# Sparse attention: index columns projected first, index scores and top 64 beside the other columns, probabilities scaled on POOL

## The chip, the cores and the metric

The kernel runs on one core of one Trainium2 chip. The metric is the device time of one execution in microseconds. The chip's engines are called as in the profile: PE (matrix), DVE (vector), ACT (scalar, activation), POOL (GpSimd), SP (which issues most DMAs). Each works through its own queue in order, and they meet on semaphores.

## What is computed

The reference is two transformer parts, one after the other. The change touches one stage of the second: the mixer `dsa_mixer` of its odd layer, for 256 tokens of width 1024, in float32. It projects the normed input to 2120 columns, rotates parts of them, and keeps 64 of up to 256 keys for each query by an index score:

```python
q, k, v, qi, ki, wi = jnp.split(proj, C_SPLITS, axis=-1)   # 1024, 256, 256, 512, 64, 8 columns
q = partial_rope(q.reshape(Bt, L, N_HEADS, HEAD_DIM), ...)  # 8 heads of 128; the first 32 are rotated
k = partial_rope(k.reshape(Bt, L, N_KV_HEADS, HEAD_DIM), ...)
qi = partial_rope(qi.reshape(Bt, L, IDX_HEADS, IDX_DIM), ...)  # 8 index heads of 64; the first 16
ki = partial_rope(ki, ...)
logits = relu(einsum('bthd,bsd->bths', qi, ki))
score = einsum('bths,bth->bts', logits, wi)                # causal mask, then top 64
_, idx = lax.top_k(score, topk)
s = q . k_sel * HEAD_DIM ** -0.5 ; pr = softmax(s) ; o = pr . v_sel
```

Only q, k and v pass through the attention itself. qi, ki and wi serve the choice of keys alone.

## The kernel before

The program is a list of stages. Each stage gives one function per engine, and `meet` makes all engines wait for each other between two stages. There is no scheduler: the order on an engine is the order in which the code is written. `sparse_attention` is the stage in question. Before and after it stand FFN stages whose time is PE's.

**Columns.** The weights come in six ring slots (`C_SLOTS`), five of 384 columns (`C_TILE`) and a last one of 256, of which 56 were in the slot before already. They are in the reference's order: q, k, v, then qi, ki, wi. To keep float32 accuracy with fp32r matmuls, each weight is split: ACT writes the high part (`high`, L1900, in two halves of four 128-row chunks), DVE the low part as a difference (`lows`, L1955), and PE makes three products for each chunk and each block of 128 tokens (L1836). So a slot is 48 matmuls. ACT copies the two finished banks (L1919) and only then makes the high part of the slot after next.

**Rotation and turning.** When all columns are copied, DVE rotates q and k (six steps of 320 elements, L1981 to L1986) and then qi and ki (six of 144), and copies ki twice side by side (L1987, L1988). Then PE transposes all 15 blocks (L1846), and ACT and DVE copy them out of PSUM by turns (L1928, L1992).

**Index and top 64.** PE makes 16 index matmuls (L1856), ACT a relu of each (L1935), DVE a weighted sum (L2000). Then for each token block DVE takes eight rounds of max and match_replace (L2008, L2009) and makes of that the additive mask `keep` (L2010, L2011).

**Head loop.** `skewed` overlaps eight heads. For a head PE makes the scores (L1863). DVE scales them and adds the mask in one pass over 512 elements (L2019), reduces to the maximum (L2022) and negates it (L2023). ACT takes the exponential with the sum on the side (L1939), DVE the reciprocal (L2029) and scales the probabilities (L2031, two of 256). PE transposes them (L1873), DVE copies (L2036), PE makes the outputs (L1883), ACT copies them (L1944). Then PE adds the residual (L1218) and the output projection (L779). POOL has no work in this stage. `pe.drain().then_inc(k.slot_freed, C_SLOTS)` behind the last column gives the six slots back, on which SP's next loads wait.

## Time and profile before

| | us |
|---|---|
| median of 3 runs | 2827.76 (2825.07 to 2828.39) |
| the profiled execution | 2824.92 |
| its span | 2823.2 |
| PE busy | 2254.3 (80%) |
| DVE busy | 878.9 (31%) |
| ACT busy | 593.7 (21%) |
| POOL busy | 63.1 (2%) |

The page's shares are means over very different stages: in the experts' part the weights' DMA sets the pace, in the FFN stages PE. What a change of one stage is worth has to be read in that stage: from its windows (busy time of each engine in a stretch), from the timeline (rows of one engine in order of time; a bracket gives the idle time before a row and who ended it), and from the chain of work that ended last.

### The profile page before, as it was taken

The page shows a single profiled execution, that of the slowest core. Times are in us where ns is not written, and L with a number is a line of the kernel's source. Part 1 is how long each engine was busy: PE and PEld are TensorE (multiplying, and loading weights), DVE is VectorE, ACT ScalarE, POOL GpSimd, SP SyncE. Part 2 cuts the span into 40 slices and gives each one's busy share as a digit, 9 for nine tenths or more (in the row PEclk, how much of TensorE's full clock was granted, in tenths as well). Part 3 has the DMA queues.
Part 4 walks back from the last instruction along what each step waited for, and adds up shares of the span by engine and source line. Part 5 has one row for each costly group of instructions (what it writes and reads, how often), then busy time and mean ns, then how long its engine had stood idle before and what let it go on. Part 6 is the DMA issues. An engine that isn't in the chain of part 4 may idle for free.

```text
span 2823.2 us, 35407 instructions
## 1 busy us (share of the span) xinstructions
PE 2254.3 (80%) x14966; PEld 1415.6 (50%) x14966; DVE 878.9 (31%) x1479; ACT 593.7 (21%) x964; POOL 63.1 (2%) x58
## 2 busy tenths in 40 slices
PE   6967776666767766776676899967999999869998
PEld 2944321222222212222221699844898799856996
DVE  5543100000000000000000454685544545573544
ACT  1411100000000000000000344201444544423443
POOL 0010000000000000000000000033000000000000
PEclk8987855665555566555655899978999999979999
DMA  5043699999999999999999754140454354232550
GB/s 231 1 167 144 268 425 425 425 425 426 425 425 425 426 425 425 425 426 426 425 426 425 311 188 162 68 164 23 162 195 183 134 188 179 86 127 90 182 184 18
DMA packets 81108, 754.27 MB, mean 267 GB/s; under 512 B 9767, under 2 KB 9928, under 8 KB 17352
## 3 DMA queue, kind: packets, MB, share of 16 engines
q1 hardware_dynamic: 78016, 748.19, 64.8%
q10 hardware_dynamic: 3016, 5.00, 0.6%
q8 instruction: 55, 0.90, 0.1%
q14 instruction: 21, 0.17, 0.0%
HBM read 752.11 MB, written 1.05 MB: 267 GB/s over the span
## 4 chain that ended last, share of the span: by engine, by line
PE 49%; DMA 38%; DVE 9%; ACT 1%; issue 1%; DVEq 0%; POOL 0%; POOLq 0%; ACTq 0%; SPq 0%
DMA ring<-in_w_up 19%; DMA ring<-in_w_gate 18%; PE ps L1270 18%; PE ps L1281 8%; PE ps L779 3%; PE ps L988 3%; PE ps L429 2%; PE ps L1012 2%; PE ps L1836 2%; PE ps L1704 2%; PE ps L1218 1%; PE ps L997 1%; DVE work L1632 1%; PE ps L1694 1%; PE ps L537 1%
## 5 line engine op out<-in xcount | busy, mean ns | idle before, releaser
L988 PE MATMUL ps<-ring,arena 128*32 128x352 f32 x3072 | 471.8, 764 | 175.9 <-DMA ring<-in_w_gate 92.6
L1270 PEld LDWEIGHTS ps<-hsplit,w 128*128 128x128 f32 x4224 | 517.6, 192 | 6.3
L1270 PE MATMUL ps<-hsplit,w 128*128 128x256 f32 x4224 | 520.3, 283 | 0.0
L988 PEld LDWEIGHTS ps<-ring,arena 128*32 128x32 f32 x3072 | 112.4, 154 | 525.5 <-DMA ring<-in_w_gate 188.7
L1039 DVE TENSOR_TENSOR arena<-arena,ps 128x352 f32<-128x352 f32 x32 | 15.2, 518 | 835.0 <-ACT arena L1029 835.0
L1029 ACT ACTIVATE arena<-ps 128x352 f32<-128x352 f32 x32 | 13.1, 461 | 1163.3 <-PE ps L988 1163.3
L1281 PE MATMUL ps<-w,hidsplit 128*128 128x512 f32 x1056 | 255.3, 391 | 0.0
L1341 DVE TENSOR_TENSOR w<-ring,w 128x1024 fp32r<-128x1024 f32 x176 | 214.4, 1222 | 43.8 <-ACT w L1304 43.8
L1281 PEld LDWEIGHTS ps<-w,hidsplit 128*128 128x128 f32 x1056 | 192.9, 188 | 36.6
L988 PE MATMUL ps<-work,arena 128*32 128x352 f32 x1024 | 159.4, 773 | 48.8 <-DMA work<-in_w_gate 24.4
L1304 ACT ACTIVATE w<-ring 128x1024 fp32r<-128x1024 f32 x176 | 184.1, 1051 | 0.0
L1012 PE MATMUL ps<-ring,arena 128*32 128x256 f32 x1280 | 115.6, 511 | 67.5 <-DMA ring<-in_w_down 54.1
L1012 PE MATMUL ps<-work,arena 128*32 128x256 f32 x1536 | 108.3, 427 | 61.2 <-DMA work<-in_w_down 61.1
L1048 DVE COPY arena<-ps 32x256 f32 x64 | 26.9, 420 | 352.9 <-PE ps L1012 352.2
L1351 DVE TENSOR_TENSOR arena<-arena,ps 128x256 f32<-128x256 f32 x88 | 37.1, 421 | 311.7 <-ACT arena L1313 311.7
L988 PEld LDWEIGHTS ps<-work,arena 128*32 128x32 f32 x1024 | 37.9, 156 | 170.1 <-DMA work<-in_w_gate 60.4
L1313 ACT ACTIVATE arena<-ps 128x256 f32<-128x256 f32 x88 | 33.9, 385 | 390.8 <-PE ps L1270 390.8
L1012 PEld LDWEIGHTS ps<-work,arena 128*32 128x32 f32 x1536 | 54.4, 124 | 115.3 <-DMA work<-in_w_down 78.1
L1012 PEld LDWEIGHTS ps<-ring,arena 128*32 128x32 f32 x1280 | 46.2, 137 | 130.0 <-DMA ring<-in_w_down 79.9
L1346 DVE TENSOR_TENSOR w<-ring,w 128x1024 fp32r<-128x1024 f32 x88 | 107.3, 1220 | 8.4 <-ACT w L1309 8.4
L1309 ACT ACTIVATE w<-ring 128x1024 fp32r<-128x1024 f32 x88 | 93.2, 1060 | 18.0 <-PE ps L1281 18.0
L779 PE MATMUL ps<-ring,arena 128*128 128x512 f32 x192 | 84.6, 602 | 0.9 <-DVEq L143 0.9
(382 smaller groups left out, 2118.3 us busy)
## 6 DMA issues: line engine op xcount, KB each, us to landing
ring<-in_w_gate SPq DMA_DIRECT2D x96, 1408.0 KB, 35.1
ring<-in_w_up SPq DMA_DIRECT2D x96, 1408.0 KB, 35.9
ring<-in_ffn_w SPq DMA_DIRECT2D x88, 1536.0 KB, 6.4
work<-in_w_down SPq DMA_DIRECT2D x64, 1536.0 KB, 37.2
ring<-in_w_down SPq DMA_DIRECT2D x32, 1536.0 KB, 35.9
work<-in_w_up SPq DMA_DIRECT2D x32, 1408.0 KB, 32.8
work<-in_w_gate SPq DMA_DIRECT2D x32, 1408.0 KB, 32.9
ring<-in_w_down SPq DMA_DIRECT2D x32, 1024.0 KB, 35.1
```

What stands on the lines that cost most here:

```text
L429: last = pe.matmul(k.ps[:, c % 6, 0:S], w_parts(c)[i][:, kk, :], h_parts[j][:, kk, :], start=(kk == 0 and n == 0), stop=(kk == DK - 1 and ...
L779: last = pe.matmul(k.ps[:, 2 * t + half, :], mixT[:, kk, t * P:(t + 1) * P], w, start=(kk == 0 and seed is None), stop=(kk == DK - 1), ski ...
L988: last = pe.matmul(k.ps[32 * g:32 * g + CAP, 2 * w + half, 0:FH], xe[:, kk, :], slot(k, base + n)[:, g * FG + half * FH:g * FG + (half + 1 ...
L1012: last = pe.matmul(k.ps[32 * j:32 * j + CAP, 6, 0:256], hidT[:, m, 32 * g:32 * g + CAP], slot(k, base + n)[:, (i - first) * D + j * 256:(i ...
L1270: last = pe.matmul(k.ps[:, 4 + c % 4, w * S:(w + 1) * S], k.w13[:, b, w, i, kk, :], k.hsplit[:, j, kk, :], start=(kk == 0 and n == 0), sto ...
L1281: last = pe.matmul(k.ps[:, 2 * t + half, :], k.hidsplit[:, b, i, t * P:(t + 1) * P], k.w2[:, b, j, half * 512:(half + 1) * 512], start=Fal ...
L1304: act.activation(k.w13[:, c % 2, w, 0], raw(c, w), ACT.Copy).then_inc(w13_high, 1)
L1309: act.activation(k.w2[:, c % 2, 0], slot(k, base + c)[:, 2 * D:3 * D], ACT.Copy).then_inc(w2_high, 1)
L1341: dve.tensor_tensor(k.w13[:, c % 2, w, 1], raw(c, w), k.w13[:, c % 2, w, 0].bitcast(F32), ALU.subtract).then_inc(w13_split, 1)
L1346: dve.tensor_tensor(k.w2[:, c % 2, 1], slot(k, base + c)[:, 2 * D:3 * D], k.w2[:, c % 2, 0].bitcast(F32), ALU.subtract).then_inc(w2_split, 1)
L1704: last = pe.matmul(k.ps[:, 2 * t + half, :], k.hsplit[:, i, kk, t * P:(t + 1) * P], w_parts(kk)[j][:, half * 512:(half + 1) * 512], start= ...
L1836: last = pe.matmul(k.ps[:, (2 * n + t) % 8, 0:WIDTH[n]], h_parts[i][:, kk, t * P:(t + 1) * P], w_part(n, j)[:, kk, :], start=(kk == 0 and ...
```

## The change

The weights' columns are put in the order qi, ki, wi, k, v, q, in six slots of 320, 264 and four times 384 columns, with none twice. What only needs the index columns moves forward:

- DVE rotates the index part after slot 1; PE transposes its five blocks behind chunk 5 of slot 2; ten of the 16 index matmuls stand in slot 3 and six in slot 4, two behind a chunk. ACT has the relus between its copies and high parts.
- DVE takes the top 64 after the last weighted sum, with one low half, (5, 1), between the two token blocks. `keep` lies in another buffer now.
- POOL gets the rotations of k, of q0 and q1, and of q2 to q4, and three low halves: both of slot 4 and the first of slot 5. DVE rotates q5 to q7 after the top 64.
- All blocks are copied out of PSUM by ACT. k, q0 and q1 are transposed before slot 5, q2 and q3 behind it, and the last two pairs behind the scores of heads 0 and 1 and DVE's rotation. The column matmuls use four PSUM banks instead of eight, the index and the turned blocks the other four.
- In the head loop one fused instruction for each token block (`tensor_tensor_reduce`) scales by the negative factor, subtracts, and takes the minimum; the exponential has scale -1. POOL scales the probabilities.
- `k.w_highs` counts the high parts apart from the low ones, because the two numbers differ now.

PE at the end of the columns, before: the last column matmul, all transposes, all index matmuls, then the scores.

```order
L1836 MATMUL ps<-c_high,c_hT_low 128x256
L1846 MATMUL ps<-arena 128x128 x30
L1856 MATMUL ps<-arena 128x128 x8
L1856 MATMUL ps<-arena 128x256 x8
L1863 MATMUL ps<-arena 128x256 x6
```

PE now, around the last chunks with index matmuls in slot 4 (L1888), and below from the last column matmul of slot 5 (L1864) on: transposes (L1904) and scores (L1911).

```order
L1888 MATMUL ps<-arena 128x256 x2
L1864 MATMUL ps<-c_high,c_hT_high 128x384
L1864 MATMUL ps<-w_low,c_hT_high 128x384
L1864 MATMUL ps<-c_high,c_hT_low 128x384
L1864 MATMUL ps<-c_high,c_hT_high 128x384
L1864 MATMUL ps<-w_low,c_hT_high 128x384
L1864 MATMUL ps<-c_high,c_hT_low 128x384
L1888 MATMUL ps<-arena 128x256 x2
```

```order
L1864 MATMUL ps<-c_high,c_hT_low 128x384
L1904 MATMUL ps<-arena 128x128 x4
L1911 MATMUL ps<-arena 128x256 x4
L1904 MATMUL ps<-arena 128x128 x8
L1911 MATMUL ps<-arena 128x256 x2
```

The index matmuls have moved in among the columns; behind the columns 12 of the 30 transposes are left beside the scores. ACT before the first exponential, before the change: the last copies, the relus, the table.

```order
L1928 ACTIVATE arena<-ps 128x256 x7
L1935 ACTIVATE arena<-ps 128x128 x8
L1935 ACTIVATE arena<-ps 128x256 x8
L1939 ACT_TABLE_LOAD
L1939 ACTIVATE arena<-arena 128x256 x6
```

ACT now: the high part of slot 5, copies of columns (L1981) and of turned pairs (L1997), and the table behind the last pair.

```order
L1969 ACTIVATE c_high<-ring 128x1536 x2
L1981 ACTIVATE arena<-ps 128x384 x2
L1997 ACTIVATE arena<-ps 128x256 x4
L1981 ACTIVATE arena<-ps 128x384 x2
L1997 ACTIVATE arena<-ps 128x256 x6
L2033 ACT_TABLE_LOAD
L2033 ACTIVATE arena<-arena 128x256 x6
```

The load of the table stood behind the relus and had the top 64 beside it; now it stands behind the copies that the last heads wait for. The diff, cut:

```diff
+C_WIDTH = [320, 264, 384, 384, 384, 384]
...
-    tmp = [work(k, 1024 + 320 * i, 320) for i in range(4)]
+    tmp = [work(k, 1024 + 144 * i, 144) for i in range(4)]
+    tmp_pool = [work(k, 1600 + 96 * i, 96) for i in range(4)]
+    keep = work(k, 2048, 512, t=ST)
...
+    POOL_LOWS = {(4, 0): 2, (4, 1): 3, (5, 0): 5}
...
     def tensor(pe):
...
+        columns(0)
+        columns(1)
+        columns(2, turn_index)
+        columns(3, index_early)
+        columns(4, index_late)
+        pe.wait_ge(q["relu_put"], ST * IH)
+        pe.wait_ge(q["pool_put"], 4)
+        turn_pair(0)
+        turn_pair(1)
+        columns(5)
+        pe.drain().then_inc(k.slot_freed, C_SLOTS)
+        pe.wait_ge(q["pool_put"], 6)
+        turn_pair(2)
+        pe.wait_ge(q["copied"], B["copied"] + ST * C_SLOTS)
+        pe.wait_ge(q["turned_put"], INDEX_TURNS + 2)
         scores(0)
-        skewed(QH, lambda h: scores(h + 1) if h + 1 < QH else None, turn, outputs)
+        scores(1)
+        pe.wait_ge(q["vector_put"], 2)
+        turn_pair(3)
+        pe.wait_ge(q["turned_put"], INDEX_TURNS + 3)
+        turn_pair(4)
+        pe.wait_ge(q["turned_put"], INDEX_TURNS + 5)
+        skewed(QH, lambda h: scores(h + 1) if 1 <= h < QH - 1 else None, turn, outputs)
...
     def scalar(act):
...
+        copies(0)
+        high(2)
+        copies(1)
+        high(3)
...
+        copies(2)
+        high(4)
+        relus(0, 10)
+        copies(3)
+        relus(10, 16)
+        high(5)
+        copies(4)
+        pair_put(0)
+        pair_put(1)
+        copies(5)
+        for i in range(2, 5):
+            pair_put(i)
...
     def vector(dve):
...
+            if t == 0:
+                lows(5, 1)
         step(dve.tensor_copy(keep[:, 0, P:S], causal_sb[:, 0, P:S]))
+        dve.wait_ge(q["copied"], B["copied"] + ST * C_SLOTS)
+        rope(dve, step, tmp, 5 * HD, 3, HD, 0, 16).then_inc(q["vector_put"], 1)
...
-            dve.scalar_tensor_tensor(out=s[:, h % 4], in0=k.ps[:, b, :].rearrange("p (t s) -> p t s", t=ST), scalar=scale,
-                                     in1=keep, op0=ALU.mult, op1=ALU.add).then_inc(q["score_read"], 1)
-            dve.wait_ge(q["score_read"], B["score_read"] + h + 1)
-            step(dve.tensor_reduce(neg, s[:, h % 4], AX, ALU.max))
-            dve.tensor_scalar(neg, neg, -1.0, None, ALU.mult).then_inc(q["score_put"], 1)
...
+            for t in range(ST):
+                dve.tensor_tensor_reduce(s[:, h % 4, t, :], k.ps[:, h % 2, t * S:(t + 1) * S], keep[:, t, :], -scale, 3e38,
+                                         ALU.add, ALU.min, neg(h)[:, t:t + 1]).then_inc(q["score_read"], 1)
...
+    def gpsimd(pool):
+        step = k.pool_order.on(pool)
+        pool.wait_ge(q["sin_done"], B["sin_done"] + 2)
+        pool.wait_ge(q["copied"], B["copied"] + 6)
+        rope(pool, step, tmp_pool, QH * HD, KVH, HD, 0, 16).then_inc(q["pool_put"], 1)
+        for half in range(2):
+            split_low(pool, 4, half).then_inc(q["pool_put"], 1)
+        pool.wait_ge(q["copied"], B["copied"] + 8)
+        pool.wait_ge(q["pool_put"], 1)
+        rope(pool, step, tmp_pool, 0, 2, HD, 0, 16).then_inc(q["pool_put"], 1)
+        split_low(pool, 5, 0).then_inc(q["pool_put"], 1)
+        pool.wait_ge(q["copied"], B["copied"] + 10)
+        pool.wait_ge(q["pool_put"], 4)
+        rope(pool, step, tmp_pool, 2 * HD, 3, HD, 0, 16).then_inc(q["pool_put"], 1)
+        for h in range(QH):
+            pool.wait_ge(q["vector_put"], 2 + h + 1)
             for t in range(ST):
...
+                pool.tensor_scalar(s[:, h % 4, t, :], s[:, h % 4, t, :], total(h)[:, t:t + 1], None,
+                                   ALU.mult).then_inc(q["p_put"], 1)
```

## Rows read from the trace of the kernel before

**Rows 1.** Chain that ended last: start us, us, engine, output, line, count.
```profile
2431.91 48.98 PE ps L1836 x285
...
2545.81 3.84 PE ps L1218 x32
```

**Rows 2.** Windows of the stage: busy us of each engine, granted clock, DMA.
```profile
core 0: us, PE busy (x) PEld busy (x) DVE busy (x) ACT busy (x) POOL busy (x), PEclk, DMA share, GB/s
2431.91:2481.23 49.32, 49.31 (x288) 48.96 (x288) 22.00 (x29) 21.25 (x33) 0.00 (x0) 0.97 0.00 1
2481.23:2502.90 21.67, 11.33 (x67) 10.08 (x67) 14.66 (x38) 9.02 (x28) 0.00 (x0) 0.77 0.96 393
2502.90:2518.39 15.49, 2.17 (x6) 1.18 (x4) 14.19 (x54) 0.00 (x0) 0.00 (x0) 0.50 0.07 27
2518.39:2545.81 27.42, 21.06 (x88) 15.52 (x89) 22.34 (x56) 11.73 (x41) 0.00 (x0) 0.84 0.00 1
```

**Rows 3.** Timeline in the columns, ACT and DVE: start, us, engine, line, operation.
```profile
2449.81 1.02 ACT L1919 ACTIVATE arena<-ps 128x384 f32<-128x384 f32 x2 [4.21 <-PE ps L1836]
...
2458.24 1.02 ACT L1919 ACTIVATE arena<-ps 128x384 f32<-128x384 f32 x2 [4.66 <-PE ps L1836]
...
2460.66 3.43 DVE L1955 TENSOR_TENSOR w_low<-ring,c_high 128x1536 fp32r<-128x1536 f32 x2 [5.00 <-ACT c_high L1900]
```

**Rows 4.** Timeline of DVE, first rotation steps of the wide and the narrow kind.
```profile
2481.70 0.49 DVE L1981 TENSOR_TENSOR work<-arena,work 128x320 f32<-128x320 f32 x1 [10.62 <-ACT arena L1919]
...
2484.85 0.31 DVE L1981 TENSOR_TENSOR work<-arena,work 128x144 f32<-128x144 f32 x1
```

**Rows 5.** Timeline from the index matmuls to the first scores read.
```profile
2494.24 3.65 PE L1856 MATMUL ps<-arena 64*128 64x128 f32 x32 [0.72 <-DVE arena L1992]
...
2499.10 4.02 DVE L2000 SCALAR_TENSOR_TENSOR arena<-arena 128x256 f32<-128x256 f32 x7
...
2503.15 0.29 DVE L2008 MAX8 arena<-arena 128x8 f32<-128x128 f32 x1
...
2509.48 0.43 DVE L2008 MAX8 arena<-arena 128x8 f32<-128x256 f32 x1
...
2518.39 0.69 DVE L2019 SCALAR_TENSOR_TENSOR arena<-ps,arena 128x512 f32<-128x512 f32 x1
```

**Rows 6.** Timeline of ACT: copies of turned blocks, load of a table.
```profile
2491.16 0.66 ACT L1928 ACTIVATE arena<-ps 128x256 f32<-128x256 f32 x2 [1.05 <-PE ps L1846]
...
2501.26 1.28 ACT L1939 ACT_TABLE_LOAD   x1
```

**Rows 7.** Timeline of the head loop: first head, one later head, last head.
```profile
2522.30 0.71 PEld L1873 LDWEIGHTS ps<-arena 128*128 128x128 f32 x4 [1.80 <-DVE arena L2031]
...
2531.74 0.57 PEld L1873 LDWEIGHTS ps<-arena 128*128 128x128 f32 x4
...
2533.09 0.68 DVE L2036 COPY arena<-ps 128x512 f32<-128x512 f32 x1
...
2533.69 0.15 DVE L2029 RECIPROCAL arena<-arena 128x2 f32<-128x2 f32 x1
...
2533.83 0.73 PEld L1883 LDWEIGHTS ps<-arena 128*128 128x128 f32 x4 [0.81 <-DVE arena L2036]
...
2534.58 0.57 PEld L1873 LDWEIGHTS ps<-arena 128*128 128x128 f32 x4
...
2542.61 0.57 PEld L1873 LDWEIGHTS ps<-arena 128*128 128x128 f32 x4
```

**Rows 8.** Groups of POOL by line and form: busy us, mean ns, idle before.
```profile
L976 POOL COPY arena<-arena 128x256 f32 x16 | 6.4, 402 | 1279.7 <-PE ps L988 1155.4 <-PEq L979 124.2
...
L559 POOL TENSOR_TENSOR work<-arena 128x512 f32<-128x512 f32 x2 | 2.5, 1266 | 171.4 <-DVE arena L586 171.4
...
L1658 POOL TENSOR_TENSOR arena<-arena 128x512 f32<-128x512 f32 x2 | 3.3, 1642 | 0.0
```

**Rows 9.** Groups of DVE by line and form: the fused product with accumulator.
```profile
L349 DVE CUSTOM_DVE_ANT_0 arena<-arena 128x1024 f32<-128x1024 f32 x2 | 2.5, 1225 | 5.8 <-DMA arena<-in_x 5.8
```

More of the change, by code:

```diff
@@ L78 @@
 W_IN_TILES = 24
-C_TILE = 384
-C_SLOTS = 6
+C_WIDTH = [320, 264, 384, 384, 384, 384]
+C_SLOTS = len(C_WIDTH)
+C_FIRST = [sum(C_WIDTH[:_n]) for _n in range(C_SLOTS)]
 C_HT_LOW = 8336
@@ L1849, in tensor, with turn_index @@
[L1849 to L1851 removed]
+                between(kk)
+        def turn_index(kk):
+            if kk != 5:
+                return
+            pe.wait_ge(q["vector_put"], 1)
+            for i, (_, at) in enumerate(INDEX):
+                for t in range(ST):
+                    src = ki2[:, t, :] if at is None else pr[:, t, at:at + P]
+                    last = pe.transpose(k.ps[:, 4 + i // 2, (i % 2) * S + t * P:(i % 2) * S + (t + 1) * P], src, k.ident)
+                if i % 2 or i == len(INDEX) - 1:
+                    last.then_inc(q["turned"], 1)
@@ L1857, in tensor, with index_early, index_late, turn_pair @@
                       start=True, stop=True).then_inc(q["index_done"], 1)
-        pe.wait_ge(q["relu_put"], ST * IH)
+        def index_early(kk):
+            if kk >= 3:
+                index(2 * (kk - 3))
+                index(2 * (kk - 3) + 1)
+        def index_late(kk):
+            if kk < 3:
+                index(10 + 2 * kk)
+                index(11 + 2 * kk)
+        def turn_pair(i):
+            for j, (_, at) in enumerate(PAIRS[i]):
+                for t in range(ST):
+                    last = pe.transpose(k.ps[:, PAIR_BANK[i], j * S + t * P:j * S + (t + 1) * P], pr[:, t, at:at + P], k.ident)
+            last.then_inc(q["turned"], 1)
@@ L1898, in high, with copies, relus, pair_put @@
             for half in range(2):
-                rows = slice(4 * half, 4 * half + 4)
-                act.activation(w_part(n, 0)[:, rows], by_chunk(slot(k, base + n), n)[:, rows], ACT.Copy).then_inc(w_high, 1)
+                act.activation(w_part(n, 0)[:, rows(half)], by_chunk(slot(k, base + n), n)[:, rows(half)],
+                               ACT.Copy).then_inc(w_high, 1)
+        PLACES = ((0, W + ID, pr, WIDE, 1.0), (W + ID, W + ID + IH, wi, 0, IH ** -0.5 * ID ** -0.5),
+                  (584, 840, pr, QH * HD, 1.0), (840, 1096, v, 0, 1.0), (1096, C_IN, pr, 0, 1.0))
+        def copies(n):
+            for t in range(ST):
+                act.wait_ge(q["column_done"], B["column_done"] + 2 * n + t + 1)
+                for c0, c1, to, at, factor in PLACES:
+                    a0, a1 = max(c0, C_FIRST[n]), min(c1, C_FIRST[n] + C_WIDTH[n])
+                    if a0 < a1:
+                        last = act.activation(to[:, t, at + a0 - c0:at + a1 - c0],
+                                              k.ps[:, 2 * (n % 2) + t, a0 - C_FIRST[n]:a1 - C_FIRST[n]], ACT.Copy, scale=factor)
+                last.then_inc(q["copied"], 1)
+        def relus(first, last):
+            for i in range(first, last):
+                t = i // IH
+                act.wait_ge(q["index_done"], i + 1)
+                if i >= 4:
+                    act.wait_ge(q["relu_used"], i - 3)
+                act.activation(relu[:, i % 4, 0:P * (t + 1)], k.ps[:, 4 + i % 4, 0:P * (t + 1)],
+                               ACT.Relu).then_inc(q["relu_put"], 1)
+        def pair_put(i):
+            act.wait_ge(q["turned"], INDEX_TURNS + i + 1)
+            for j, (to, _) in enumerate(PAIRS[i]):
+                last = act.activation(to, k.ps[:, PAIR_BANK[i], j * S:(j + 1) * S], ACT.Copy)
+            last.then_inc(q["turned_put"], 1)
         for kk in range(DK):
@@ L1950, in vector, with lows @@
         step = k.vector_order.on(dve)
-        def lows(n):
-            for half in range(2):
-                rows = slice(4 * half, 4 * half + 4)
-                dve.wait_ge(w_high, w_before + 2 * n + half + 1)
-                dve.tensor_tensor(w_part(n, 1)[:, rows], by_chunk(slot(k, base + n), n)[:, rows],
-                                  w_part(n, 0)[:, rows].bitcast(F32), ALU.subtract).then_inc(w_split, 1)
+        def lows(n, half):
+            split_low(dve, n, half).then_inc(w_split, 1)
         for kk in range(DK):
@@ L2044, in second @@
+    return Stage(tensor, scalar, vector, gpsimd)
 def second(k, t, base, out):
```

202 lines of the change are left out of this document (91 added, 111 removed).

## The prediction

> **What bounds the kernel now.** I read the chain that ended last first: in this stage it is the projection matmuls on PE, and the chain comes back to PE for long only with the mixer's residual matmuls at 2545.81 [rows 1]. What lies between is a relay. The table of windows shows it [rows 2]: while the columns run (2431.91 to 2481.23) PE is full, DVE and ACT are each busy under half of the time, and POOL does nothing. In the next 21.7 us the rotation, the transposes and the index scores pass from one engine to another. Then DVE alone picks the top 64 for 15.5 us, with PE at half of its clock (granted 0.50). Then comes the loop over eight heads, with DVE the busiest (22.3 of 27.4 us). So 64.6 us stand between the last column and the residual, and DVE has room beside the columns. Behind the stage stand an FFN and the last gate stage with the same instructions as before, in which PE sets the pace: what the stage gains, the end gains. The transfers that wait for the columns' ring slots fill the window after them (DMA share 0.96 over 21.7 us [rows 2]); they will start some 4 us later, near 2486, and be in by about 2508, before the residual even at its new place (2519.6).
>
> **Durations, and how far they carry.** The sum is made against the profiled execution, 2824.92 us (span 2823.2). It is 2.84 us below the median of the runs, 2827.76; I carry the difference over to that median.
>
> **The columns on PE.** A slot of 384 columns lasts from 2449.81 to 2458.24, so 8.43 us [rows 3]. The six slots had 2176 columns in all (56 of them twice) and now have 2120: 56/384 of 8.43 is -1.2 us. The first slot is 320 wide instead of 384, so its first high and low halves are a sixth shorter; DVE's pair took 3.43 in the wide form [rows 3], so one half saves 0.29, and ACT's half about as much: PE starts 0.5 us earlier, at 2431.4. Inserted among the matmuls are 10 transposes for the index (0.14 each by the pitch of the head loop's four in 0.57 [rows 7], 1.4 us), 16 index matmuls (3.65 us all together [rows 5], partly at half clock, so an upper bound) and 8 transposes for k and q0, q1 (1.1 us). The last column then ends at 2481.23 - 0.5 - 1.2 + 1.4 + 3.65 + 1.1 = 2485.7, and its copy at about 2486.8.
>
> **When the top 64 can start.** The last six index matmuls stand in slot 4 behind chunk 2. Up to slot 2 the old schedule was at 2458.24; one more slot makes 2466.7. Take off the 0.5 and 184 columns (4.0 us), add the 10 transposes (1.4) and ten early index matmuls (2.2): slot 4 starts at 2465.8. Three of its eight chunks (3.2) and the late index matmuls (1.4) give 2470.4. DVE follows with one weighted sum per 0.57 us (7 in 4.02 [rows 5]) and is behind because ACT copies slot 3 between the tenth and the eleventh relu: I take 1.5 us, so 2471.9.
>
> **DVE's own chain.** Top 64 of block 0 takes 2509.48 - 2503.15 = 6.33 us, block 1 and the last copy 2518.39 - 2509.48 = 8.91 us [rows 5]. Between them now stands one low half (1.72 [rows 3]), which PE needs at chunk 4 of slot 5 and gets at about 2480.0; slot 5 reaches chunk 4 at about 2481.5. Then the rotation of q5 to q7: six steps of 96 elements, against 0.49 at 320 and 0.31 at 144 [rows 4], so 0.27 and a small gap each, 1.7 us. The sum: 2471.9 + 6.33 + 1.7 + 8.9 + 1.7 = 2490.6. There DVE reads the first scores; before it did so at 2518.39. **27.8 us earlier.** PE's copied columns (2486.8) leave 2 us of room, so the end of the path is DVE's.
>
> **What is new on the way to the first head.** In the old kernel 2522.30 - 2518.39 = 3.9 us pass from there to the first transposes of probabilities [rows 5, 7]. Now PE turns the last two pairs of q only after the rotation (0.8 us until the first is done), ACT copies them (0.66 each, as for two blocks before [rows 6]) until 2493.0, and only behind them in ACT's queue stands the load of the exponential's table, 1.28 us, which before lay under the top 64 (2501.26 [rows 6]). So the first exponential starts at 2494.3, both are done at 2495.5, then reciprocal 0.2 and POOL's two scalings 0.9 with a handover: transposes at 2496.6. That is 6.0 us instead of 3.9, a loss of 2.1; the first transposes come 25.7 us earlier.
>
> **The head loop.** DVE loses the reduce, the negation and the two scalings and gets two fused reads with a minimum. One such instruction of 1024 elements took 1.225 us [rows 9]; at one element per 1.04 ns (the difference between 0.49 at 320 and 0.31 at 144 is 0.18 for 176) 256 elements take 0.43, and I allow 0.5 with the accumulator's read. Its bounds are 0.31 (144 elements, rows 4) and 0.69 (one read of 512 elements [rows 5]). Two make 1.0 us, no longer the limit: DVE has about 1.9 us a head. What limits is a ring through four engines: four transposes with their depth 0.8, copy 0.68, reciprocal 0.15 [rows 7], POOL's two scalings, and five handovers of 0.05 to 0.1. **POOL's scaling is in no row.** Below it is bounded by POOL's copy of 256 elements, 0.40 [rows 8]; above by half of its two-input product of 512 elements with DVE at work, 1.64/2 = 0.82 [rows 8]. A gain beyond that is excluded: the copy is the cheapest pass of this width that POOL shows. I take 0.43, nearest to the copy, since both read one tensor. The ring is then 0.8 + 0.68 + 0.15 + 0.86 + 0.25 = 2.74 us, against 2.84 (2531.74 to 2534.58 [rows 7]). The old loop takes 20.3 us from first to last transposes (2522.30 to 2542.61), in which the first three heads take 9.4 us in place of 8.5 (to 2531.74), PE's clock being low there, and the last two 0.5 less. Seven rings of 2.74 and the early 0.9: 20.2, a gain of 0.1; with a ring of 2.65 it is 0.8. I take 0.5.
>
> The Trainium skill, GPSIMD Engine Reference, in its table on engine selection, speaks against this part: elementwise work belongs on VectorE, GpSimd being about twice as slow with two inputs, though roughly at line rate with one. The trace agrees on both: the 512-element product takes 1.27 us on POOL [rows 8] against 0.69 of a DVE pass of that size [rows 5], and the copy 0.40. By the first half of that rule for the scaling the sum is the first rival's, by the second half it is mine.
>
> **POOL's other work** has cover, if the rows carry. A low half of 1536 elements on POOL is three times the 512-element product: 3.8 (1.27 each) to 4.9 us (1.64 each) [rows 8]. The rotations are six steps of 64 or 96 elements in runs of 16; between 0.1 and 0.8 us each, I take 0.42 (the copy). Slot 2 ends at about 2455.4 (2458.24 - 0.5 - 4.0 + 1.4, and small gaps) and is copied, in two pieces a block, by 2457.0: rotation of k to 2459.5, low(4,0) to 2463.4, low(4,1) to 2467.3, needed by PE at 2465.8 and 2471.3. Rotation of q0, q1 to 2471.2, low(5,0), whose high half ACT gives at 2472.5, to 2476.4, needed at 2477.0. At 4.9 us a half it is 2477.4: 0.4 us of PE's 2 us of room. With rotations of 0.8 and halves of 4.9 about 1.5 us come through. I take nothing, at most 2.
>
> **Sum.** -25.7 to the first transposes, -0.5 in the loop, nothing behind it: -26.2. 2824.92 - 26.2 = 2798.7 for a profiled execution, and **2801.5 us** for the median.
>
> **Rivals.**
> 1. *POOL's scaling becomes the loop's limit.* At 0.82 each the ring is 0.78 longer: 7 x 0.78 + 0.8 in the lead-in = 6.3 us back, 2807.8; at 0.62, 2804.6. For it: no row shows the form, it reads a scalar per partition as well. Against: the copy's 0.40. 20%.
> 2. *PE stands in front of POOL's halves or the index relay is slower than I laid it out* (ACT's queue mixes copies, relus and halves; DVE's sums wait for it). It costs 2 to 5 us: 2803.5 to 2806.5. For: room of only 0.6 us before slot 5. 12%.
> 3. *It gains more.* If the lead-in costs nothing and the loop falls to what PE needs (weight loads of 0.57 for the transposes, 0.73 for the outputs and as much for the scores, with gaps about 2.3 us [rows 7]), 2.1 and 2.6 us more: 2796.8. 10%.
> 4. *It does not do what it says*: the top 64 starts only when the columns are out (a wait that I read wrongly in one of the queues). DVE's 15.2 us then stand behind 2485.7 instead of 2471.9: 13.8 us back, 2815.3. In the order of instructions nothing on DVE stands between the last sum and the first maximum. 3%.
> 5. *Slower than before.* POOL's low halves are far slower than three products, for their output type or the 4-row pattern, and PE waits in the middle of slots 4 and 5. To lose the 26 us, low(5,0) must come 26 + 2 + 0.6 us late, and three halves lie ahead of it: 28.6/3 = 9.5 us more each, 13.4 us in place of 3.9. DVE's same product with this output type takes its 1.72 for 1536 as any, so I see nothing for it. 2%.
>
> The forecast itself has 53%. The range must hold eight in ten: from 2796.0 (rival 3) to 2810.0 (rival 1 at its bound and 2 us of rival 2). A measurement of this kernel can tell about 0.2%, 5.7 us, from no change. The forecast and rivals 1 to 4 are all faster by more than that and hold 0.98; I take 3 in 100 off them for what no row shows, and give 0.02 to the same and 0.01 to slower beside rival 5: faster 0.95, the same 0.02, slower 0.03.
>
> **What would show it.** Right: the first fused read on DVE starts 27 to 29 us earlier than 2518.39; PE has no wait of over 0.5 us within slots 2 to 5; POOL's 1536-element product takes 3.8 to 4.9 us; a head takes 2.6 to 2.8 us; between the first fused read and the first transposes lie about 6 us with the table load on ACT. Wrong: a POOL scaling of over 0.6 us (rival 1), PE idle on a POOL product at slot 4 or 5 (rivals 2 and 5), a DVE gap before the first maximum beyond 2475 (rivals 2 and 4), or columns at half clock because of the pauses between them.

## The result, and the profile after

| | before | after |
|---|---|---|
| median of the runs, us | 2828.39 (2825.07 to 2831.44, 5 runs) | 2811.14 (2806.55 to 2814.56, 5 runs) |
| profiled execution, us (span) | 2824.92 (2823.2) | 2811.34 (2809.6) |
| stage: first ACT copy of hT | 2428.19 | 2428.01 |
| from there to the output projection behind the residual | 121.3 | 107.5 |

The ratio is 0.9936, 95% interval 0.9922 to 0.9949: faster by 0.6%, that is 17 us by the medians and 13.6 us by the profiled executions, where 26 were forecast. 2811.14 lies 1.1 us above the upper end of the range. All of the 13.6 lies in this stage: 13.8 us within it, and the start and what follows it move by 0.4 us at most.

The chain that ended last, from DVE's last rotation step to the residual (start us, us, engine, output, line, count). It answers to [rows 7] and to the second row of [rows 1]:

```profile
2492.95 0.27 DVE arena L1842
...
2493.27 1.98 PE ps L1904 x8
...
2495.27 0.66 ACT arena L1997 x2
2495.95 1.28 ACT L2033
2497.24 1.10 ACT arena L2033 x4
...
2498.37 0.18 DVE arena L2111
...
2498.63 1.83 POOL arena L2139 x2
...
2500.51 1.13 PE ps L1921 x4
...
2514.69 0.67 PE ps L1921 x4
...
2515.39 0.04 DVE arena L2117
2515.43 0.57 issue
2515.99 0.17 DVE arena L2111
...
2516.24 1.84 POOL arena L2139 x2
...
2518.12 0.67 PE ps L1921 x4
...
2529.89 5.76 PE ps L1219 x32
```

From 2514.69 to 2518.12 one head goes by: transposes 0.67, DVE's copy (0.04 and the 0.57 named issue, in which DVE is still busy with it), reciprocal 0.17, POOL's scaling 1.84, and the gaps: 3.43 us, of which more than half is POOL's. In [rows 7] a head takes 2.84. The residual matmuls take 5.76 instead of 3.84 [rows 1].

POOL's scaling is one group (busy us, mean ns):

```profile
L2139 POOL TENSOR_SCALAR arena<-arena 128x256 f32<-128x256 f32 x16 | 14.6, 925 | 27.9 <-DVE arena L2111 27.9
```

Windows of the stage, to set beside [rows 2]: lead-in to the first turned head, head loop, residual.

```profile
core 0: us, PE busy (x) PEld busy (x) DVE busy (x) ACT busy (x) POOL busy (x), PEclk, DMA share, GB/s
...
2493.13:2500.51 7.38, 4.04 (x12) 2.74 (x12) 2.39 (x14) 5.75 (x17) 1.82 (x2) 0.50 1.00 424
2500.51:2529.89 29.38, 22.32 (x84) 14.76 (x84) 9.91 (x35) 7.98 (x29) 12.78 (x14) 0.79 0.33 140
2529.89:2535.49 5.60, 5.60 (x32) 5.60 (x33) 0.00 (x0) 1.25 (x1) 0.00 (x0) 0.64 0.00 0
```

The old relay of 21.7 us and the 15.5 us of selection behind it [rows 2] are gone: the first maximum starts at 2474.26, beside the columns, and the first scores are read at 2493.13 instead of 2518.39. Then 11 us are given back: the lead-in takes 7.4 us (3.9 before), the loop to the residual 29.4 (2522.30 to 2545.81, 23.5, before), the residual 5.6 (3.7). The granted clock is 0.50 in the lead-in, that is 1.2 GHz, and 0.64 in the residual.

One more thing shows that was not forecast. Timelines of DVE and POOL at the weighted sums (start, us, engine, line, operation), with DVE's waits for the last relus:

```profile
2458.59 6.96 POOL L1829 TENSOR_TENSOR w_low<-ring,c_high 128x1536 fp32r<-128x1536 f32 x2
...
2460.52 1.69 DVE L2080 SCALAR_TENSOR_TENSOR arena<-arena,work 128x128 f32<-128x128 f32 x1 [8.01 <-ACT arena L1991]
2462.33 6.11 DVE L2080 SCALAR_TENSOR_TENSOR arena<-arena 128x128 f32<-128x128 f32 x7
...
2471.28 1.08 DVE L2080 SCALAR_TENSOR_TENSOR arena<-arena 128x256 f32<-128x256 f32 x2 [0.53 <-ACT arena L1991]
2473.15 1.07 DVE L2080 SCALAR_TENSOR_TENSOR arena<-arena 128x256 f32<-128x256 f32 x2 [0.80 <-ACT arena L1991]
...
2480.75 1.91 DVE L1829 TENSOR_TENSOR w_low<-ring,c_high 128x1536 fp32r<-128x1536 f32 x1
...
2481.13 1.78 POOL L1842 TENSOR_TENSOR arena<-work 128x96 f32<-128x96 f32 x1
```

The same sums by line (ns, shortest, median and longest):

```profile
L2080 DVE SCALAR_TENSOR_TENSOR arena<-arena x14: 351/483/3373, 2462.3 to 2473.7; 128x128 f32<-128x128 f32 x7, 128x256 f32<-128x256 f32 x7
```

POOL's first low half ends at 2462.06. DVE's first sum, started at 2460.52, ends at 2462.21, 0.15 later; its second, the first of the seven in the row, starts at 2462.33 and takes 3.37 us, to 0.15 behind the end of POOL's second half (2465.55). A sum of that width takes 0.35 to 0.41 otherwise. At 2481.13 it is the other way round: POOL's rotation step takes 1.78 us instead of 0.40, and ends 0.25 us after DVE's low half. So here one of the two stands until the other's instruction is done. The Trainium skill, SBUF — State Buffer, sections "SBUF: two separate sides" and "Who interferes with whom", says just this: DVE with two SBUF inputs and a GpSimd instruction that reads SBUF share a port pair under an exclusive lock, held for the whole instruction. The trace agrees, and the forecast had not used that rule. DVE makes up for the hold, though: before its last two pairs of sums it waits 0.53 and 0.80 us for ACT's relus, and these for TensorE's index products.

### The profile page after: what moved, and what is told of

Same layout as the page of the kernel before. It is cut to its first block, busy times and chain, and to the rows that moved or that the text cites. A ratio compares the mean times of both kernels' runs of the same rounds, so it can differ in the third digit from the quotient of the medians.

```text
span 2809.6 us, 35462 instructions
## 1 busy us (share of the span) xinstructions
PE 2256.8 (80%) x14966; PEld 1412.9 (50%) x14966; DVE 863.1 (31%) x1460; ACT 594.6 (21%) x974; POOL 96.4 (3%) x95
## 3 DMA queue, kind: packets, MB, share of 16 engines
HBM read 751.88 MB, written 1.05 MB: 268 GB/s over the span
## 4 chain that ended last, share of the span: by engine, by line
PE 49%; DMA 38%; DVE 9%; ACT 1%; issue 1%; POOL 1%; DVEq 0%; POOLq 0%; ACTq 0%; SPq 0%
DMA ring<-in_w_up 19%; DMA ring<-in_w_gate 18%; PE ps L1271 18%; PE ps L1282 8%; PE ps L780 3%; PE ps L989 3%; PE ps L430 2%; PE ps L1013 2%; PE ps L1705 2%; PE ps L1864 1%; PE ps L1219 1%; PE ps L998 1%; DVE work L1633 1%; PE ps L1695 1%; PE ps L538 1%
## 5 line engine op out<-in xcount | busy, mean ns | idle before, releaser
L989 PE MATMUL ps<-work,arena 128*32 128x352 f32 x1024 | 159.4, 773 | 48.9 <-DMA work<-in_w_gate 24.5
```

Of the source, the lines that this page charges most:

```text
L989: last = pe.matmul(k.ps[32 * g:32 * g + CAP, 2 * w + half, 0:FH], xe[:, kk, :], slot(k, base + n)[:, g * FG + half * FH:g * FG + (half + 1 ...
```

## The experiments

They ran on three chips, each beside runs of the kernel before on its chip (medians 2826.07 to 2827.93). The stage starts at 2426.5 to 2433.9 us in the profiled executions, with nothing changed ahead of it; why is open. So besides the median the table gives distances within the stage of one profiled execution, us from its first ACT copy: first maximum, first scores read, first turned head (T0), residual (R), output projection (O).

| kernel | median us | ratio, 95% interval | max | read | T0 | R | O |
|---|---|---|---|---|---|---|---|
| before | | 1 | 75.0 | 90.2 | 94.1 | 117.6 | 121.3 |
| after | 2811.14 | 0.9936 (0.9922 to 0.9949) | 46.3 | 65.1 | 72.5 | 101.9 | 107.5 |
| scale_dve | 2797.78 | 0.9903 (0.9888 to 0.9918) | 46.1 | 64.9 | 71.0 | 92.2 | 95.8 |
| low4_dve | 2811.40 | 0.9947 (0.9933 to 0.9960) | 46.0 | 64.9 | 72.3 | 100.6 | 104.3 |
| scale_low4 | 2801.34 | 0.9910 (0.9895 to 0.9925) | 46.1 | 64.9 | 71.0 | 92.2 | 95.9 |
| scale_low4_table | 2798.27 | 0.9896 (0.9881 to 0.9912) | 46.2 | 65.1 | 69.8 | 90.1 | 93.7 |
| pool_probe | 2810.3 (one) | | 46.1 | 65.4 | 72.9 | 102.7 | 107.7 |
| index4 | 2809.07 | 0.9936 (0.9919 to 0.9952) | 46.3 | 65.7 | 72.3 | 101.7 | 107.4 |
| index4_low4 | 2804.76 | 0.9924 (0.9907 to 0.9940) | 41.3 | 60.0 | 66.6 | 96.4 | 101.2 |
| best | 2790.18 | 0.9874 (0.9857 to 0.9890) | 41.3 | 60.0 | 63.9 | 83.5 | 87.2 |
| before_pool_scale | 2830.84 | 1.0012 (1.0003 to 1.0022) | 75.1 | 90.3 | 95.6 | 123.1 | 126.8 |
| pool_tt | 2804.37 | 0.9919 (0.9901 to 0.9936) | 46.3 | 65.1 | 71.8 | 94.8 | 98.5 |
| scale_split | 2803.58 | 0.9911 (0.9893 to 0.9929) | 46.3 | 65.1 | 71.8 | 94.8 | 98.5 |
| best_tt | 2794.26 | 0.9882 (0.9863 to 0.9900) | 41.5 | 60.2 | 64.6 | 87.7 | 91.4 |

The intervals of scale_dve, scale_low4_table, best and best_tt lie clear below that of the changed kernel; those of low4_dve, scale_low4, index4, index4_low4, pool_tt and scale_split overlap it, and best and best_tt overlap each other. There the distances carry the verdict. Where nothing ahead of a mark was changed they agree to 0.3 us.

The theory: the loop is long because POOL's scaling is (925 ns, not 430) and stands in each head's ring; the selection is late because POOL's low halves hold DVE's sums. Rivals: the loop is slow for another reason (the fused reads, where the tiles lie, the clock, the next weights' transfers beside it); the selection waits for the index products.

**scale_dve: the scaling back on DVE.** POOL's loop over the heads goes; the diff, cut:

```diff
-            dve.reciprocal(total(h), total(h)).then_inc(q["vector_put"], 1)
+            step(dve.reciprocal(total(h), total(h)))
+            for t in range(ST):
+                dve.tensor_scalar(s[:, h % 4, t, :], s[:, h % 4, t, :], total(h)[:, t:t + 1], None, ALU.mult).then_inc(q["p_put"], 1)
...
```

> The changed kernel with the probabilities scaled on DVE again, all else as changed. In the changed kernel POOL's two scalings take 1.82 us a head and the head's ring is 3.43 us. Theory A (POOL's scaling sets the ring): DVE's pair takes 0.62, the ring falls to what DVE and PE need, 2.4 to 2.6 us, so 7 x 0.9 = 6 us, 1.2 us in the lead-in, and 1.9 us at the residual if PE's clock stays up through the loop: 8 to 10 us faster than the changed kernel, 2801 to 2803. Theory B (DVE becomes the limit as it was in the kernel before): ring 2.84, 4 us + 1.2: 2804 to 2806. Theory C (the loop is not where the gain went): within 2 us of the changed kernel, 2809 to 2813.

Windows of this kernel: the loop from first to last transposes, and the residual.

```profile
2497.57:2515.51 17.94, 16.37 (x76) 12.95 (x77) 13.80 (x52) 8.40 (x31) 0.00 (x0) 0.90 0.62 261
...
2518.71:2522.38 3.67, 3.67 (x32) 3.67 (x33) 0.00 (x0) 1.25 (x1) 0.00 (x0) 1.00 0.00 0
```

The seven heads take 17.9 us instead of 24.9, 2.56 each in the mean, and the residual is at full clock. The stage is 11.7 us shorter, more than the 8 to 10 expected, because the seven heads give 7.0 and not 6 and what follows them runs at full clock too (3.2 us, not 4.45); the median is 13.4 lower. The rest of the changed kernel, its fused reads too, is as it was. The scaling on POOL is the loss.

**before_pool_scale: that part alone, in the kernel before.** POOL's two products a head stand in the place of DVE's; the sums get room for four heads.

> One part of the change alone: the kernel before, in which POOL and not DVE scales the probabilities (two 256-column products a head, sums kept for four heads). Everything ahead of the head loop stays. In the changed kernel POOL's pair takes 1.82 us a head and the loop advances by 3.43 us a head where it had 2.74 to 2.9. Theory A (the product on POOL is slower by 1.2 us a head than DVE's 0.62 and stands in the ring of each head): the head loop takes 24 to 26 us from first to last turn instead of 20.3, and the kernel is slower than before by 4 to 8 us with what a colder TensorE clock adds at the residual products. Theory B (the forecast's: POOL frees DVE and the loop runs at 2.74): faster by 0.5 us. Theory C (the loop of the changed kernel is slow for another reason, for instance where its sums and probabilities lie): no change here.

```profile
2536.25 1.83 POOL L2043 TENSOR_SCALAR arena<-arena 128x256 f32<-128x256 f32 x2 [1.61 <-DVE arena L2029]
```

The same pair (1.83) and the same pitch (1.83 and 1.61 idle: 3.43 or 3.44), with the old reads and, but for the sums, the old tiles: 24.5 us over seven heads instead of 20.3, 5.5 us more in the stage. The kernel is slower by 0.12% (interval 0.03 to 0.22), 2.9 us by the medians, less than the 4 to 8 expected; that is below the forecast's own bound for a difference, so the stage's distances carry the verdict. DVE freed of its work bought nothing.

**pool_probe: what the product costs on POOL.** Ten more instructions on scratch columns, while POOL waits for the first head.

> The changed kernel with ten extra POOL instructions on scratch columns, put while POOL waits for the first head's sums: a tensor_scalar product by a per-partition value at 64, 128, 256 and 512 columns, the same by the constant 0.5 at 128, 256 and 512, and a plain copy at 128, 256 and 512. Nothing of the computation changes; the time should stay that of the changed kernel, since POOL is idle there for 15.7 us. In the changed kernel the per-partition product took 925 ns at 256 columns where a POOL copy of that width took 402. Theory A (the product runs column by column at a slower pace than a copy, about 3.3 to 3.6 ns a column): 64 / 128 / 256 / 512 take about 0.25 / 0.47 / 0.92 / 1.8 us and the constant one about the same as the per-partition one. Theory B (reading the per-partition value costs a fixed 0.5 us): the constant one takes 0.40 to 0.45 at 256, and the per-partition one 0.7 / 0.8 / 0.92 / 1.3 at the four widths. Theory C (it was slow only because DVE and ACT worked on the same head's columns beside it): at least one of these, with fewer neighbours, takes 0.4 to 0.5 at 256.

Groups by form: L2140 by a per-partition value, L2142 by a constant, L2144 a copy.

```profile
L2140 POOL TENSOR_SCALAR work<-work,arena 128x512 f32<-128x512 f32 x1 | 1.6, 1565 | 0.1
L2142 POOL TENSOR_SCALAR work<-work 128x512 f32<-128x512 f32 x1 | 1.5, 1488 | 0.1
L2140 POOL TENSOR_SCALAR work<-work,arena 128x256 f32<-128x256 f32 x1 | 0.9, 925 | 0.1
L2142 POOL TENSOR_SCALAR work<-work 128x256 f32<-128x256 f32 x1 | 0.8, 848 | 0.1
L2144 POOL COPY work<-work 128x512 f32<-128x512 f32 x1 | 0.6, 613 | 0.1
...
L2140 POOL TENSOR_SCALAR work<-work,arena 128x64 f32<-128x64 f32 x1 | 0.4, 444 | 0.1
L2144 POOL COPY work<-work 128x256 f32<-128x256 f32 x1 | 0.4, 401 | 0.1
```

From 256 to 512 columns the product grows by 640 ns, 2.5 ns a column; the copy by 212, 0.83 a column. The per-partition value costs 75 to 77 ns over a constant. 925 at 256 is the same here as in the loop, so it isn't the neighbours on the same head that make it slow. The changed kernel itself shows it once more with its last pair:

```profile
2523.56 1.83 POOL L2139 TENSOR_SCALAR arena<-arena 128x256 f32<-128x256 f32 x2 [2.07 <-DVE arena L2111]
```

Over these 1.83 us DVE and ACT do nothing at all. Theory A holds in the main, but with 2.5 ns a column instead of 3.3 to 3.6, and with about 0.28 us fixed that it did not have. The copy was the wrong row to be nearest to: it is three times as fast a column.

**pool_tt and scale_split: two shorter scalings.** The first makes the pair one two-input product, the second gives block 0 to DVE and block 1 to POOL.

```diff
-            for t in range(ST):
-                pool.tensor_scalar(s[:, h % 4, t, :], s[:, h % 4, t, :], total(h)[:, t:t + 1], None,
-                                   ALU.mult).then_inc(q["p_put"], 1)
+            pool.tensor_tensor(s[:, h % 4], s[:, h % 4], total(h).unsqueeze(2).to_broadcast([P, ST, S]),
+                               ALU.mult).then_inc(q["p_put"], ST)
```

> The changed kernel with the two POOL products of a head made one product with two inputs over 512 columns, the reciprocal read again for every column. In the trace of the kernel before POOL's two-input product of 512 columns took 1266 ns alone and 1642 ns with DVE beside it; the two one-input products take 1824 ns together. Theory A (what counts is the time of POOL's step in each head's ring): 0.2 to 0.55 us a head less, a ring of 2.9 to 3.2 us instead of 3.43 and 2 to 4 us less in all. Theory B (a two-input product on POOL keeps DVE's two-input operations waiting, as its low halves did): DVE's fused reads and copies in the loop grow by up to 1 us each and the ring is no shorter or is longer, 2811 to 2820.

> The changed kernel with a head's scaling shared: DVE scales the first block (0.31 us), POOL the second (0.92 us) at the same time. Theory A (the ring is set by the longer of the two plus the hand-over): the wait behind the reciprocal falls from 1.82 to 0.95 us a head, the ring from 3.43 to 2.55 to 2.7, and the time to between DVE scaling both (10.6 us less than the changed kernel by the medians then taken) and the changed kernel: 2801 to 2806. Theory B (POOL's product is slow because DVE works beside it and grows further when both scale the same head): the POOL product takes over 1.1 us and the ring stays above 3.0.

POOL in the loop of pool_tt, then of scale_split:

```profile
2512.95 1.04 POOL L2138 TENSOR_TENSOR arena<-arena 128x512 f32<-128x512 f32 x1 [1.66 <-DVE arena L2111]
```

```profile
2512.64 1.08 POOL L2140 TENSOR_SCALAR arena<-arena 128x256 f32<-128x256 f32 x1 [1.61 <-DVE arena L2111]
```

Both give a pitch of 2.7 us in the later heads (2.86 in the mean over seven) and 23.0 us from T0 to R, just what the forecast had laid out for a scaling of 0.86 a head. The two-input product of 512 columns takes 1.04, so less than two one-input ones (1.82), and less than I expected from [rows 8]. DVE was not held in pool_tt: its fused reads kept 421 ns (422 in the changed kernel) and its copies 692 (691); each of them has one input in PSUM. In both, theory A stands: what counts is POOL's step in the ring. pool_tt gains 9.0 us in the stage, far more than the 2 to 4 expected, because its product is shorter than the rows had it and the residual runs at full clock; scale_split falls in its range. In scale_split POOL's product grew from 925 to 1080 ns beside DVE's, the direction of theory B, but not its size.

At 2.7 another ring holds. The chain of pool_tt goes through two heads:

```profile
2507.55 1.05 POOL arena L2138
...
2508.65 0.66 PE ps L1921 x4
2509.30 0.86 PE ps L1911 x4
2510.17 1.06 PE ps L1931 x4
...
2511.26 0.38 ACT arena L2038
2511.64 0.98 ACT arena L2033 x4
...
2512.65 0.17 DVE arena L2111
...
2512.95 1.05 POOL arena L2138
```

That is 5.40 us for two heads. By the forecast's own ring (transposes, copy, reciprocal, scaling) this kernel would take 3.43 - 1.84 + 1.05 = 2.64. So the two-head ring is the longer one here.

**low4_dve: slot 4's low halves on DVE, before its sums.** The diff, cut:

```diff
-    POOL_LOWS = {(4, 0): 2, (4, 1): 3, (5, 0): 5}
+    POOL_LOWS = {(5, 0): 3}
...
         lows(3, 1)
+        lows(4, 0)
+        lows(4, 1)
...
```

> The changed kernel with both low halves of slot 4 on DVE instead of POOL. In the changed kernel two of DVE's weighted sums last 1.69 and 3.37 us, each until 0.15 us after a POOL low half ends. Theory A (a DVE pass with two SBUF inputs cannot run beside a POOL pass with two): the weighted sums are back at 0.35 each, the first maximum comes 2 to 2.5 us earlier (2472 against 2474.3), and so does the stage's end: 2808 to 2809.5. Theory B (the sums wait for the relus and PE, not for POOL): the first maximum stays at 2474 or goes later by DVE's added 3.4 us, 2811 to 2815.

```profile
2461.51 0.41 DVE L2082 SCALAR_TENSOR_TENSOR arena<-arena,work 128x128 f32<-128x128 f32 x1
2462.03 0.35 DVE L2082 SCALAR_TENSOR_TENSOR arena<-arena 128x128 f32<-128x128 f32 x1
...
2464.20 0.81 DVE L2082 SCALAR_TENSOR_TENSOR arena<-arena 128x128 f32<-128x128 f32 x2 [0.87 <-ACT arena L1991]
```

The sums are free (0.35 to 0.41 instead of up to 3.37), but now each pair waits 0.8 to 1.2 us for ACT, which waits for TensorE: two index products come each 1.67 us (each 1.88 for the second token block). The first maximum stays where it was, as theory B had it, and the median too. So my expectation of an earlier selection fell; a second limit stood at the same height as the first.

**index4 and index4_low4: the other limit, and both.** Four index products to a chunk, behind chunks 3 to 6 of slot 3, none in slot 4, all relus ahead of slot 3's copies. The diff, cut:

```diff
-            if kk >= 3:
-                index(2 * (kk - 3))
-                index(2 * (kk - 3) + 1)
+            if 3 <= kk < 7:
+                for i in range(4 * (kk - 3), 4 * (kk - 3) + 4):
+                    index(i)
...
```

> The changed kernel with the sixteen index products put four to a contraction step (steps 3 to 6 of column 3) instead of two, and the relus all ahead of column 3's copies. POOL keeps its low halves. In the changed kernel and in the one where DVE makes column 4's low halves the first maximum starts 46.2 and 46.0 us after the stage's first ACT copy, though in the second no sum is held up. Theory A (two limits stand behind one another: TensorE hands out two index products every 1.67 us, and beside it POOL's two low halves hold DVE's sums for about 5 us): with the denser products alone the first maximum comes at most 2 us earlier, since the sums are still held. Theory B (only the pace of the index products sets it): the first maximum comes 5 to 6 us earlier. Either way the scores are read from 0 to 2 us earlier, since the last column ends at 59.1 us after the stage's first copy and its copies and rotation follow; time 2809 to 2812.

> Both together: four index products to a contraction step, and column 4's two low halves on DVE ahead of its sums instead of on POOL beside them. Theory A of the run with denser products alone (two limits, one behind the other): the first maximum comes 40 to 42 us after the stage's first ACT copy instead of 46.0, and the first fused score read about 2 us earlier than in the changed kernel (63.2 instead of 65.1 after that copy), where the last column's copies and its rotation on DVE become what it waits for; time about 2809. Theory B: the same first maximum as with the denser products alone.

Alone it moves the first maximum by 0.1 us, to later, and the first read by 0.6; with the low halves off POOL by 5.0 us, and the first read with it (60.0 instead of 65.1). Each limit was hidden by the other. In index4 the hold even reaches TensorE, as its chain shows:

```profile
2467.04 3.35 DVE arena L2077
...
2470.48 0.29 ACT arena L1989
...
2470.81 2.13 PE ps L1888 x4
2472.94 2.22 PE ps L1864 x6
```

DVE's sum is held for 3.35 us, ACT's relu waits for its buffer, TensorE waits 1.92 us for the relu and then runs at half clock (granted 0.50 from 2471 to 2477): the last column matmul starts 63.1 us after the stage's start instead of 59.1. In index4_low4 it starts at 57.4: four interruptions of the columns instead of eight save 1.7 us, about 0.4 each. I had expected the read at 63.2 and 2809 us there, not 60.0 and 2804.8. DVE waits only 0.16 us for the last column's copy, so the selection and the last column are through at almost the same time, both earlier.

**scale_low4, scale_low4_table.** scale_low4 joins the first two edits. The other has beside it one dummy exponential on ACT behind the third pair's copy (`act.activation(m[:, 39:40], k.ident[:, 0:1], ACT.Exp)`), so that the table is loaded while DVE is still at the top 64.

> Both of the two edits before. If the two causes are separate and lie one behind the other on the path, the gains add: 10 to 12 us under the changed kernel, about 2799 to 2801. If PE's wait before slot 5 takes over when the top 64 starts earlier, no more than the larger of the two.

> As scale_low4, and one exponential of a single column put on ACT behind the third pair of copies, so that the table is loaded while ACT is idle (5.5 us idle there in the changed kernel). Theory: the load of 1.28 us leaves the way to the first exponential, 1.3 us less, 2797.5 to 2800. Rival: the copies behind it load another table again, then nothing or 1.3 us more.

scale_low4 equals scale_dve within the stage (95.9 and 95.8), as low4_dve would have it; the sum of two gains that I expected first did not come. The early table brings the first exponential from 4.1 to 2.7 us behind the first read, 1.4 us, and the seven heads from 17.9 to 17.1. In all the stage is 2.2 us shorter, where 1.3 were expected.

**best and best_tt.** All four edits, and the same with POOL's two-input product instead of DVE's scaling.

> All that the runs so far speak for: DVE scales the probabilities as in the kernel before, the exponential's table is loaded after the third pair's copies instead of ahead of the first exponential, column 4's low halves on DVE, and four index products to a step. The kernel with the first three takes 93.7 us from the stage's first ACT copy to the output projection, the changed kernel 107.5. If the first fused read now comes 2 us earlier, 91.5 to 92 us, and 2796 by the median (the kernel before less 29 to 31 us). If the last column's copies and pairs were the limit already, nothing beyond the 93.7 and 2798.

> The fastest kernel so far (table load behind the third pair's copies, column 4's low halves on DVE, four index products to a step, DVE scaling; 87.2 us from the stage's first ACT copy to the output projection, 2790.2 us) with the scaling back on POOL, as one two-input product of 512 columns (1.04 us where the changed kernel's two one-input products take 1.82). Theory A (in this loop the scaling is part of each head's ring on whichever engine it runs, and DVE's 0.62 us for the pair is shorter than any form on POOL): the loop advances by 2.70 us a head as with this product in the changed kernel, against 2.34 here, first to last turn 19 to 20 us instead of 16.4, and 2793 to 2794 by the median. Theory B (freeing DVE shortens the ring once POOL's step is short): 16.4 us or less, and 2790 or less.

Windows of best: lead-in and loop.

```profile
2488.24:2492.15 3.91, 2.36 (x14) 1.53 (x12) 2.38 (x13) 3.77 (x14) 0.00 (x0) 1.00 1.04 427
2492.15:2508.55 16.40, 14.82 (x76) 11.42 (x77) 13.71 (x52) 8.39 (x31) 0.00 (x0) 1.00 1.01 430
```

More than expected: the read comes 5.1 us earlier than in scale_low4_table, not 2, and the lead-in and the heads are 1.5 us shorter besides, at a clock of 1.00. best beats both kernels: 2790.18, ratio 0.9874 (0.9857 to 0.9890), 21 us below the changed kernel by the medians and 20.3 in the stage. Its loop runs with a DMA share of 1.01, so the transfers beside it don't make a loop slow. Its last column ends within a microsecond of the end of the selection, so TensorE does not pause for long; the clock stays at 1.00 and the lead-in is 3.9 us as in the old kernel. A head takes 2.34 us, in the chain transposes 0.44, scores 0.87, outputs 1.05, all TensorE. With the shortest scaling of a pair seen on POOL (best_tt) the heads take 2.86 in the mean and the kernel 4.1 us more by the medians, whose intervals overlap (4.2 within the stage): here too the scaling is dearer on POOL. The pitch of its later heads is the expected 2.70; the first ones are longer.

## Why the forecast was wrong, step by step

The forecast's times, less the 2428.19 of the old stage start, stand against the changed kernel's distances. By profiled executions it missed by 2811.34 - 2798.7 = 12.6 us (9.6 by the medians).

- **First maximum** (43.7 forecast, 46.3 measured): 2.5 us late. The term that failed is "16 index matmuls (3.65 us all together ..., so an upper bound)". Among the columns a pair of products with the return to the columns costs 1.67 or 1.88 us less the 1.05 of its six column matmuls, so four times 0.62 and four times 0.83, 5.8 us together; the last product ends at 2472.7, not at the forecast's 2470.4. DVE is then 1.5 us behind, as forecast. POOL's halves took 3.5 us, even less than the 3.8 to 4.9 forecast; what they cost is DVE's standing still, which the forecast did not have. In the changed kernel that hold is made good by the end of the sums, so taking it away alone gave nothing (low4_dve), and neither did the denser products alone, since then the hold sets the pace (index4); both together give 5.0 us (index4_low4). So this is part of rival 2, by a mechanism that it does not name.
- **From there to the first read** 18.9 us, forecast 18.7. Right, as was the order: DVE's chain ended the path, not the columns, although these ended 1.9 us later than forecast (59.4, not 57.5), for the same 5.8 instead of 3.65 us. index4_low4 shows where the price lies: about 0.4 us for each interruption.
- **Lead-in** 7.4 us, forecast 6.0. The table load, 1.28 us behind the last pair, was where I put it. Of the 1.4 missing, 1.0 is POOL's pair (1.83, not 0.86), the rest the eight transposes at half clock (1.98 us in the chain). Their price was taken from matmuls at full clock, though TensorE had then stood for 3.2 us.
- **The loop** from T0 to the residual 29.4 us, forecast 23.0. **This is the step that failed**: "I take 0.43, nearest to the copy", and "above by half of its two-input product ... 0.82". It measured 0.925, above the upper bound. The bound supposed that a pass with one input can't be dearer than one with two; pool_probe and pool_tt show that it is. The ring itself was right: with 1.84 a head it is 3.43. That pool_tt has T0 to R of 23.0, as forecast, is in part luck: with 0.86 and the other terms as measured the forecast's ring would be 2.45, and the two-head ring, 2.70 a head with pool_tt's 1.05 and some 2.6 with 0.86, would have set the pace. Term by term of a head: scaling 1.84 for 0.86, but transposes 0.67 for 0.8, the copy 0.61 for 0.68, gaps 0.14 for 0.25, the reciprocal 0.17 for 0.15, so 3.43 for 2.74. Seven heads are 4.8 us of the 6.4; 1.25 fall behind the last transposes, where the granted clock was 0.50 (4.45 us instead of 3.2), and the rest into the first and the last of the seven (3.89 each). The forecast's own sum for the loop has a slip, 7 x 2.74 + 0.9 is 20.1 and not 20.2; nothing hangs on it.
- **Residual** 5.6 us, forecast 3.7 as before, because the granted clock was 0.64; TensorE had run at 0.50 since 2520.6, through most of the last two heads. In low4_dve the seven heads are as slow as here (25.3 us against 24.9) and yet the clock is at 1.00 from the last transposes on; from there to the output projection it needs 6.7 us and the changed kernel 10.1. So about 3 us of the profiled execution are the clock's. Every kernel with 2.7 us a head or less ran the residual at 1.00; of those at 3.43 two did (low4_dve, before_pool_scale) and four did not. What decides between these is open.

2.5 + 0.2 + 1.4 + 6.4 + 1.9 is 12.4 of the 12.6. Of the rivals, the first came true beyond its bound (priced there at 6.3 us), together with the 2.5 us of the first maximum, part of the second. The range's upper end was made of just these two, and fell short by the bound and by the clock at the residual. Of its own signs of being right, TensorE had no wait in slots 2 to 5; the first fused read came 25.3 us earlier, not 27 to 29, and a head took 3.43, not 2.6 to 2.8. Its sign for rival 1, a scaling of over 0.6 us, is what the trace has. The forecast's sign and its claim that the selection goes beside the columns were right. Rival 3's 2.3 us a head, "what PE needs", is what best runs at (2.34). The rule weighed in the forecast, the Trainium skill, GPSIMD Engine Reference, section "Engine selection", holds that elementwise work belongs on VectorE; the trace agrees. Its remark that one-input work on GpSimd runs at roughly line rate does not hold for this form, a product by a value per partition: 925 ns at 256 columns, where DVE scales a pair of blocks in 0.62 us and POOL in 1.83.

## What to carry to other kernels

Freeing DVE was worth nothing here, because its work stayed in the same ring on a slower engine: ask what the step costs in the ring, not what the engine saves. Price an instruction by a row of its own form; a copy is no bound for a product, nor a two-input pass an upper bound for a one-input one. And where a cause is removed and nothing moves, look for the second limit at the same height before dropping the first: to the first read low4_dve gained 0.2 us and index4 lost 0.6, the two together gained 5.2.

## What the runs showed of the hardware that was not expected

- On POOL a product by a per-partition value takes 444, 603, 925 and 1565 ns at 64, 128, 256 and 512 columns; a copy 289, 401 and 613 at the last three; one two-input product over 512 columns with a repeated second input 1040.
- POOL's two-input instructions from SBUF and DVE's two-input instructions from SBUF did not run together: a DVE sum of 0.35 us took 3.37, a POOL rotation step of 0.40 took 1.78, each until about 0.15 to 0.25 us after the other's end.
- Such a hold can travel: DVE, ACT, TensorE, and then the clock. In index4, with a held sum of 3.35 us, the last column matmul starts 4.0 us later than in the changed kernel and 5.7 later than in index4_low4, which has the same products and no hold.
